# Head norms of q and k on ScalarE out of PSUM, and four modulation chunks moved between the projections

## The reference

```
mod = silu(cond) @ mod_w + mod_b                     # 6 x 1024, one for context, one for latent tokens
h = rmsnorm(x, g) * (1 + scale_m) + shift_m
a_val, a_gate, q, k, v = split(h @ in_w)             # 512, 512, 8 x 128, 2 x 128, 2 x 128
a = silu(layernorm(depthwise_conv31(a_val * sigmoid(a_gate)) + conv_b))
q = rmsnorm(q, q_norm_g); k = rmsnorm(k, k_norm_g)   # over each head's 128 values
q, k = rope(q), rope(k)                              # latent tokens only; context k, v are outputs
o = softmax(q @ [k_cache, k]^T / sqrt(128)) @ [v_cache, v]
x = x + gate_m * (concat(a, o) @ out_w)
x = x + gate_f * moe(...)                            # 16 experts, top 2 of one group
```

## Time and profile before

| | us |
|---|---|
| median of 3 runs | 1434.71 |
| the profiled execution | 1433.41 |
| its span, first to last instruction | 1431.6 |

### The profile page before, as it was taken

How to read it: one execution, slowest core, us unless ns; L and a number is a source line. 1 busy time by engine, 2 the same in 40 slices (tenths; PEclk the granted TensorE clock), 3 DMA queues, 4 the chain that set the end, 5 groups by cost and what they waited for, 6 DMA issues and landing times. The chain is left out here.

```text
span 1431.6 us, 14569 instructions
## 1 busy us (share of the span) xinstructions
PE 1298.0 (91%) x5682; PEld 725.5 (51%) x5682; DVE 536.2 (37%) x1045; ACT 286.1 (20%) x627; POOL 135.8 (9%) x139
## 2 busy tenths in 40 slices
PE   4999788988999989795999999999999979999886
PEld 1543345445544534241577775777586454454332
DVE  0268686143000012432543554455655550000044
ACT  2110244032111110101421220220223131011122
POOL 0069900000000010000110100000100000000010
PEclk9999999998999999997999999999999989999998
DMA  9617599642999992801222323233224927999994
GB/s 398 276 59 316 224 427 430 285 176 100 401 426 425 427 426 104 352 1 59 74 82 95 125 74 133 74 125 118 74 81 152 385 103 297 428 426 426 427 424 189
DMA packets 34793, 344.38 MB, mean 241 GB/s; under 512 B 3856, under 2 KB 8976, under 8 KB 15760
## 3 DMA queue, kind: packets, MB, share of 16 engines
q1 hardware_dynamic: 22608, 315.34, 53.5%
q0 software_dynamic: 4608, 16.78, 3.0%
q10 hardware_dynamic: 7488, 11.01, 2.1%
HBM read 324.51 MB, written 18.61 MB: 240 GB/s over the span
## 5 line engine op out<-in xcount | busy, mean ns | idle before, releaser
L722 PE MATMUL PS<-ring,hT 128*64 128x512 f32 x896 | 243.6, 610 | 18.4 <-PEq L848 4.8
L532 PE MATMUL PS<-ring,hT 128*128 128x512 f32 x432 | 191.4, 597 | 0.0
L722 PEld LDWEIGHTS PS<-ring,hT 128*64 128x64 f32 x896 | 85.0, 141 | 147.7 <-issue 144.6
L532 PEld LDWEIGHTS PS<-ring,hT 128*128 128x128 f32 x432 | 82.0, 192 | 99.2 <-issue 98.5
L734 PE MATMUL PS<-ring,area 128*64 128x512 f32 x448 | 114.9, 603 | 10.0 <-issue 5.7
L1812 DVE TENSOR_TENSOR area<-area,PS 128x512 f32<-128x512 f32 x16 | 11.0, 687 | 301.6 <-PE PS L722 301.5
L887 PE MATMUL PS<-ring 128*128 128x256 f32 x480 | 108.7, 379 | 1.2 <-ACT ring L1296 1.2
L722 PE MATMUL PS<-area,hT 128*64 128x512 f32 x256 | 99.7, 626 | 10.9 <-DMA ring<-moe_w_up 4.9
L887 PEld LDWEIGHTS PS<-ring 128*128 128x128 f32 x480 | 91.1, 190 | 14.0 <-issue 1.6
L868 PE MATMUL PS<-ring,area 128*128 128x512 f32 x192 | 83.8, 593 | 3.8 <-ACT area L1384 3.8
L743 PEld LDWEIGHTS PS<-area 128*128 128x128 f32 x672 | 81.1, 202 | 11.8 <-issue 11.8
(11 more groups left out here) (271 smaller groups left out, 1456.4 us busy)
## 6 DMA issues: line engine op xcount, KB each, us to landing
ring<-moe_w_gate SPq DMA_DIRECT2D x25, 2048.0 KB, 16.8
ring<-mod_w SPq DMA_DIRECT2D x24, 2048.0 KB, 19.2
ring<-moe_w_down SPq DMA_DIRECT2D x24, 2048.0 KB, 21.9
ring<-moe_w_up SPq DMA_DIRECT2D x24, 2048.0 KB, 19.1
ring<-in_w SPq DMA_DIRECT2D x21, 2048.0 KB, 7.8
area<-moe_w_up SPq DMA_DIRECT2D x8, 2048.0 KB, 21.1
area<-moe_w_down SPq DMA_DIRECT2D x8, 2048.0 KB, 23.9
ring<-out_w SPq DMA_DIRECT2D x7, 2048.0 KB, 8.0
```

Source lines behind the costliest of these rows:

```text
L532: mm = pe.matmul(out, lhs(k), rhs(k), start=n == 0, stop=n == KD - 1)
L722: mm = pe.matmul(PS[64 * e:64 * e + 64, j, :], g[:, k, 64 * e:64 * e + 64], W[e][:, k, :], start=k == 0, stop=k == KD - 1)
```

## The change

1. **Head norms.** ACT squares each head of a tile straight out of PSUM with an accumulated sum, takes the root, waits for DVE's reciprocal (new semaphore `qk_inv`), and copies each head out of PSUM scaled by it. DVE's square, reduce and both multiplies are gone. Its rotation uses tables in which the norm's weights are already multiplied (`qk_cos`, `qk_sin`, in slot 5, built once before the gated products); on context tiles, which have no rotation, the multiply by the weight stays.
2. **Taps.** They are handed out in a new order: 28 as before, then four in each of the nine tiles (36), and the 29 left are spread over the 25 attention steps (two in each of the first four, then one).
3. **Modulation.** `MODS_BEHIND` puts 12 chunks behind the nine tiles (1, 1, 2, 1, 2, 1, 2, 1, 1), the last four of them layer 1's first. The eight left of layer 1 follow every third head. The PSUM banks for them change (`mod_bank`).
4. **Gate rows** follow tiles 7 and 8 in place of 6 and 7; ACT copies the first step ahead of tile 8 and the second behind it.
5. **Slots** of the five are no longer taken in turn: each matrix gets the slot whose last use comes first in the order of uses.

The parts of `rope`'s signature and its caller in layer 1 that only pass tables are left out here.

```diff
+MODS_BEHIND = [[(0, 4)], [(0, 5)], [(0, 6), (0, 7)], [(0, 8)], [(0, 9), (0, 10)], [(0, 11)], [(1, 0), (1, 1)], [(1, 2)], [(1, 3)]]
+MODS_BEHIND = [[("mod", l, c) for l, c in m] for m in MODS_BEHIND]
+MODS_ATTENTION = [("mod", 1, c) for c in range(MODS, 3 * MODS)]
+PRE_TAPS, QK_TAPS = 7, 4
+
+def plan_taps():
+    left, order, prior = {}, [], None
+    for n in range(3 * TAPS):
+        for b in range(3):
+            if n == PRE_TAPS * b:
+                left[b] = 0
+        b = min((b for b in left if left[b] < TAPS), key=lambda b: (b == prior, left[b], b))
+        order.append((b, left[b]))
+        left[b] += 1
+        prior = b
+    return order
...
-    for n, (kind, layer, c) in enumerate(first):
-        put(kind, layer, [c], [n % 5])
+    use = [("mod", 0, c) for c in range(MODS)] + [("in", 0, 0), ("in", 0, 1)]
+    for n in range(3 * TT):
+        use += [("in", 0, 2 + n // TT)] + MODS_BEHIND[n]
+    use += MODS_ATTENTION + [("out", 0, c) for c in (1, 2, 0)]
+    first = sorted(set(use), key=use.index)
+    done = {key: max(n for n, k in enumerate(use) if k == key) for key in first}
+    held = [None] * 5
+    for key in first:
+        i = min(range(5), key=lambda i: -1 if held[i] is None else done[held[i]])
+        held[i] = key
+        put(key[0], key[1], [key[2]], [i])
...
+def mod_bank(g):
+    return 6 + g % 2 if g < 4 else 1 + g % 2
...
-                if n != 7:
-                    modulation(0, [4 + min(n, 7)])
-                if n == 6:
+                for _, l, c in MODS_BEHIND[n]:
+                    modulation(l, [c])
+                if n == 7:
                     gate_rows(0, (3, 4, 3, 4), [0])
-                if n == 7:
+                if n == 8:
                     pe.wait_ge(gate_copied, 2)
                     gate_rows(0, (3, 4, 3, 4), [1])
...
-                    if u % 2 == 0:
-                        modulation(1, [u // 2])
+                    if u % 3 == 0:
+                        modulation(1, [MODS + u // 3])
...
             for n in range(3 * TT):
                 c, t = n // TT, n % TT
-                if n == 3 * TT - 2:
-                    gate_copies(0, (3, 4), range(2))
+                heads = range(4 * c, 4 * c + 4) if c < 2 else range(QH, HQK)
+                r = 16 + 4 * (n % 2)
                 if n == 3 * TT - 1:
-                    gate_copies(0, (3, 4), range(2, 4))
-                    head_rms(n - 1)
+                    gate_copies(0, (3, 4), range(2))
                 act.wait_ge(proj_mm, JOBS[(0, 2 + c, t)])
...
+                for i in range(len(heads)):
+                    a = act.activation(squares[:, i * HD:(i + 1) * HD], PS[:, n % 3, i * HD:(i + 1) * HD], ACT.Square,
+                                       accum_out=stat[:, r + 8 + i:r + 9 + i])
+                a.then_inc(qk_sq, 1)
...
+                act.wait_ge(qk_sq, n + 1)
+                act.activation(stat[:, r:r + len(heads)], stat[:, r + 8:r + 8 + len(heads)], ACT.Sqrt, bias=eps,
+                               scale=1.0 / HD).then_inc(qk_rms, 1)
+                act.wait_ge(qk_inv, n + 1)
+                for i, hd in enumerate(heads):
+                    a = act.activation(qk[:, t, hd, :], PS[:, n % 3, i * HD:(i + 1) * HD], ACT.Copy,
+                                       scale=stat[:, r + i:r + i + 1])
+                a.then_inc(qk_copied, 1)
+                for _, l, c in MODS_BEHIND[n]:
+                    mod_copies(l, [c])
+            gate_copies(0, (3, 4), range(2, 4))
...
+            for i in range(2):
+                g = V[:, V_QKG + HD * i:V_QKG + HD * i + HD]
+                dve.tensor_tensor(qk_cos[:, i], C[:, C_COS:C_COS + 2 * P].rearrange("p (t n) -> p t n", t=2),
+                                  g.unsqueeze(1).to_broadcast([P, 2, P]), ALU.mult)
...
-                link(dve.tensor_tensor(ta, qk[:, t, hs], qk[:, t, hs], ALU.mult))
-                dve.tensor_reduce(stat[:, 24 + 4 * (n % 2):24 + 4 * (n % 2) + heads], ta, AX, ALU.add).then_inc(qk_sq, 1)
-                for b, j in taps[done:min(done + 2, early)]:
-                    conv_tap(b, j)
-                done = min(done + 2, early)
-                dve.wait_ge(qk_rms, n + 1)
-                link(dve.reciprocal(r, r))
-                link(dve.tensor_tensor(qk[:, t, hs], qk[:, t, hs], r.unsqueeze(2).to_broadcast([P, heads, HD]), ALU.mult))
-                i = dve.tensor_tensor(qk[:, t, hs], qk[:, t, hs], V[:, g:g + HD].unsqueeze(1).to_broadcast([P, heads, HD]),
-                                      ALU.mult)
+                dve.wait_ge(qk_rms, n + 1)
+                dve.reciprocal(r, r).then_inc(qk_inv, 1)
+                convolve(QK_TAPS)
+                dve.wait_ge(qk_copied, n + 1)
+                need(dve, qk_ready, n - 1)
...
-                for b, j in taps[2 * u:2 * u + 2]:
-                    conv_tap(b, j)
+                convolve(-(-len(taps) // (TT * QH + 1 - u)))
```

More of the change, by code:

```diff
@@ L288, in backbone_kernel @@
         tm = tmp2.rearrange("p a b c -> p (a b c)")
+        squares = slot(5)[:, 2 * D:2 * D + 4 * HD]
+        qk_cos, qk_sin = (slot(5)[:, 3 * D + 512 * i:3 * D + 512 * i + 512].rearrange("p (a t n) -> p a t n", a=2, t=2)
+                          for i in range(2))
         sig = tm[:, 0:CB * NT].rearrange("p (a b) -> p a b", a=CB)
@@ L1570, in conv_tap @@
                                                  ALU.mult, ALU.add)
-                if b == 2 and j == TAPS - 1:
+                if (b, j) == TAP_ORDER[-1]:
                     i.then_inc(conv_dve, 1)
@@ L1574, in conv_tap, with convolve @@
                     last[b] = mark(i)
-            taps = [(0, j) for j in range(7)] + [(b, j + 7 * (b == 0)) for j in range(TAPS) for b in range(2) if j + 7 * (b == 0) < TAPS]
-            early = 3 * TAPS - 2 * (TT * QH + 1)
-            done = 0
+            for i in range(2):
+                g = V[:, V_QKG + HD * i:V_QKG + HD * i + HD]
+                dve.tensor_tensor(qk_cos[:, i], C[:, C_COS:C_COS + 2 * P].rearrange("p (t n) -> p t n", t=2),
+                                  g.unsqueeze(1).to_broadcast([P, 2, P]), ALU.mult)
+                for t in range(2):
+                    sin, out = (v.rearrange("p (x y j) -> p x y j", x=2, y=2)
+                                for v in (C[:, C_SIN + P * t:C_SIN + P * t + P], qk_sin[:, i, t, :]))
+                    for y in range(2):
+                        k = dve.tensor_tensor(out[:, :, y, :], sin[:, :, y, :],
+                                              g.rearrange("p (x y j) -> p x y j", x=2, y=2)[:, :, 1 - y, :], ALU.mult)
+            link(k)
+            taps = list(TAP_ORDER)
+            def convolve(n):
+                for b, j in taps[:n]:
+                    conv_tap(b, j)
+                del taps[:n]
             for b in range(CB):
@@ L1586, in _ @@
                 dve.wait_ge(glu_done, b + 1)
-                for tap in taps[done:done + 7]:
-                    conv_tap(*tap)
-                done += 7
+                convolve(PRE_TAPS)
             for n in range(3 * TT):
@@ L1618, in _ @@
             dve.wait_ge(qk_ready, 3 * TT)
-            first, block2 = taps[early:], [(2, j) for j in range(TAPS)]
-            taps = [tap for pair in zip(first, block2) for tap in pair] + block2[len(first):]
             for u in range(TT * QH + 1):
```

57 lines of the change are left out of this document (20 added, 37 removed).

## The result

The changed kernel takes 1422.07 us (1419.83 to 1423.31, 4 runs), the kernel before 1434.68 us on the same chip (1431.75 to 1434.94, 4 runs): a ratio of 0.9915 with a 95% interval of 0.9896 to 0.9934. The forecast was 1424.3 in a range of 1420.5 to 1430.5. The profiled execution took 1421.28 us, its span is 1419.4.

What follows compares the result with a forecast made beforehand. PE was taken to set the pace in tile stage and attention, with DVE and DMA close; -1.2 to the first scores, 0 in context heads, -8.6 in latent heads and -0.6 at the end made -10.4: 1424.3 us, range 1420.5 to 1430.5.

Steps and rivals of the forecast that it cites:

- Tile stage: PE to the end of tile 8: gate-row wait gone -8.6, four chunks +7.4, second gate step out -1.7; -2.9 us.
- Behind tile 8: From tile 8 to the first scores: ACT starts 1.7 us later behind the second gate step; first scores at 179.4, -1.2.
- Head norms, tables: Norms moved to ACT in the tile stage, rotation tables built where DVE idles: turnaround 3.5 us, hidden, cost 0.
- The price of up to 2 us for a lost cover behind the last tile: ACT's norms behind the last tile would cost at most 2 us if chunk and gate step didn't cover them; left out of the sum.
- Ring: Weight transfers into the slots: no wait in the tile stage (bounds 0 and +5), experts' queue cost 0.
- Attention: Context heads 14.8 us as now; latent heads net -8.6 us; last head one tap less, -0.6.
- the 2.8 us of waits for DMA: PE's waits for modulation weights in the latent heads, taken to vanish with only five chunks left to come: 2.8 us saved.
- The first: Rival: attention heads without a chunk stay at about 2.3 us through handshakes; +5.5, so 1429.8 us; chance 0.17.
- The second: Rival: the tile stage waits for weight transfers, two or three chunks late; +5, so 1429.3 us; chance 0.08.
- The third: Rival: context heads also run at 1.34 us and ACT's stores don't hold up; -3.5, so 1420.8 us; chance 0.08.
- The fourth: Rival: PE's clock falls in the attention, half of it at 1.2 GHz; +22, so 1446 us; chance 0.05.
- The fifth: Rival: little effect, layer-0 experts start when they did; within 3 us of the kernel before; chance 0.05.

Runs made afterwards that it cites:

- gate_rows_old_place: The changed kernel with both gate-row steps, and ACT's copies, back behind tiles 6 and 7: 1427.03 us, 0.9966 of the kernel before.
- gate_rows_only: The kernel before with one edit, both gate-row steps one tile later (behind tiles 7 and 8): 1421.27 us, 0.9936 of the kernel before.
- stores_later: The changed kernel with ACT's four k/v stores moved behind the exponentials of heads 1 to 4: 1421.46 us, 0.9913 of the kernel before.
- norms_on_vector: The changed kernel with the norms' squares, sums and scaling back on DVE, rotation tables and four taps a tile kept: 1422.49 us, 0.9949 of the kernel before.
- slots_in_turn: The changed kernel with its new chunk order but the five slots taken in turn: 1438.22 us, 1.0046 of the kernel before.
- after_again: The changed kernel unaltered, profiled and timed once more: 1425.90 us, 0.994 of the kernel before.
- taps_in_attention: The changed kernel with taps handed out as before, 15 in the tiles and 50 in the attention: 1430.62 us, 0.999 of the kernel before.
- squares_twice: The changed kernel with each head's square issued twice on ACT, the first into a spare place: 1425.69 us, 0.9962 of the kernel before.

## Why the prediction was right

By its own steps, from tile 0 on, the forecast gave 86.5, 10.8, 14.8 and 53.2 - 8.6 - 0.6 = 44.0 us; measured are 86.1, 10.9, 14.7 and 43.8. The sum was to be -10.4; it is -11.0 at the output projection and -10.5 at the first expert.

**Tile stage.** Right: no wait before the gate rows, four chunks for 7.4, one step behind tile 8. But the price of 8.6 us hangs on the gate rows only in the kernel before. In the changed kernel the other parts remove the same wait (gate_rows_old_place), and the edit alone brings all of the gain (gate_rows_only).

**Behind tile 8.** Right to 0.2 us, with the four stores as the cause of 1.5 of it (stores_later).

**Head norms, tables.** Cost 0 was right, by the slack that the forecast read from the rows; the turnaround was 2.9 us and not 3.5, the squares 0.26 apiece and not 0.36. That the whole part is worth nothing in the changed kernel (norms_on_vector), the forecast didn't say. Nor did it say that the norms bring the diagonals of the gate rows 2.2 us sooner, which is part of why the old place no longer waits for them. The price of up to 2 us for a lost cover behind the last tile was too high: in gate_rows_old_place no gate step lies there, and ACT still issues its first store 2.1 us behind tile 8 (171.25 - 169.16), against 2.0 before.

**Ring.** No wait in the stage, as taken, and slots_in_turn shows what the slot rule is worth there: 13.8 us. The cost at the experts' queue was taken as 0, and no cost is seen: 95.7 us before and 96.2 after from output projection to expert, 93.6 in norms_on_vector with the same slots.

**Attention.** The size was right, one term of it was put down to the wrong edit: the 2.8 us of waits for DMA were credited to the chunks that leave the attention, and they go with the gate rows alone. Without them the chunk move is 7.2 us paid in the tile stage and 0.7 among the context heads for 5.2 to 5.7 saved in the latent ones. The total came right because all parts were changed at once: which of them gets the credit for a wait doesn't alter the sum. As an account of the single edits it fails. A forecast edit by edit would have been wrong in sign for this one.

**Rivals.** The first (heads at 2.3 us) is out: 7.16 us for three heads and a chunk is 1.8 a head. The second didn't come; slots_in_turn is what it would have looked like. The third didn't come by its mechanism: the context heads take 14.7 us as before and the stores do hold ACT up, though the median, 1422.07, lies nearer to its 1420.8 than to the forecast. The fourth, the clock, is real but smaller than its price of 22 us: 0 in one profile of the changed kernel, 1.6 in the other, up to the output projection. The fifth is out, for the first expert came earlier by the whole sum.

**The rest.** The median came 2.2 us under the forecast. Against the forecast the profile has 1.8 of such a difference in the opening, where tile 0 came earlier under a higher granted clock; since after_again has it at 81.94 and gate_rows_only, whose opening is the code of before, at 78.46, this is no gain of the change.

## What to carry to other kernels

Before crediting an edit with a wait, ask which other parts of the change would remove it too, and run the smallest edit alone: here a move of eight matmuls brought all of the gain of a rewrite. Before blaming an edit for a longer wait, look whether the same wait grew in kernels that don't have it: here a slow store issue and the low clock behind it stood in three variants with different edits. A step moved from one stage to another pays where it lands, so move it to where its engine stands anyway (PE among the context heads), not to where it is full. Compare by marks inside the trace: where the clock was the same they repeated to 0.1 us, while whole spans of one program differed by 5.

## What the runs showed of the hardware

The granted clock can fall in the middle of a dense kernel, in a stage of short bursts. It was at the level of 1.2 GHz for 16 us in gate_rows_old_place, at means between 0.50 and 0.81 for 4 to 20 us in gate_rows_only (0.58 from 168 to 172), taps_in_attention, squares_twice, norms_on_vector and slots_in_turn (0.79 from 196 to 204), and at 0.79 for 8 us in one profile of the changed kernel and not in the other. In the three profiles in which already the turning of q and k ran slowly, PE had stood 2.79, 2.49 and 2.10 us for ACT just before; behind 1.52 us in the changed kernel and 1.46 before, the turning ran at the full clock. The Trainium skill, "TensorE: Matmul & The Clock Gate", Part 1, puts an idle PE at half rate, and tells of a case in which short idles between groups of matmuls made the clock swing. The trace fits the second more than the first: PE was at most 2.8 us idle at a time here, and busy 7.43 of 8 us while the clock was at 0.50. What decides it between two executions of one program stays open.

The issue of a small store on ACT's queue took 0.34 to 0.61 us in most profiles, and 0.98, 1.13, 1.44 and 1.45 in three of them. ACT's next work waited for it. What makes it long stays open.
